# Seven block products for eight in two of the four FFN down units of ten groups

## The reference

```python
def conv_ffn(h, w_up, conv_w, conv_b, w_down, buf):
    z = h @ w_up
    T = z.shape[1]
    zp = jnp.concatenate([buf.astype(z.dtype), z], axis=1)
    zc = conv_b + sum(zp[:, j:j + T] * conv_w[j] for j in range(CONV_W))
    g, a = jnp.split(zc, 2, axis=-1)
    y = (jax.nn.silu(g) * a) @ w_down
    return y, zp[:, -(CONV_W - 1):]
...
    x = x + mix.astype(dt)
    f, new_buf = conv_ffn(rmsnorm(x, norm2), w_up, ffn_conv_w, ffn_conv_b, w_down, conv_buf)
    x = x + f.astype(dt)
```

## Time and profile before

| | |
|---|---|
| median of 3 runs | 2255.8 us (2255.7 to 2257.31) |
| the profiled execution's own time | 2254.32 us |
| its span, first to last instruction | 2252.5 us |
| mean granted TensorE clock | 0.997 |
| TensorE busy in the span | 2227.6 us (99%) |
| matmuls | 18338 |

### The profile page before, as it was taken

The page is one execution under the profiler, slowest core; times in us unless marked ns, Lnnn a source line. Parts: engine busy times, 40 slices in busy tenths (PEclk is TensorE's granted clock), DMA queues, the critical chain, the costliest instruction groups (busy, mean ns, idle before and its releaser), DMA issues.

```text
span 2252.5 us, 44763 instructions
## 1 busy us (share of the span) xinstructions
PE 2227.6 (99%) x18338; PEld 2166.1 (96%) x18338; DVE 876.1 (39%) x1428; ACT 736.5 (33%) x1257; POOL 940.5 (42%) x748
## 2 busy tenths in 40 slices
PE   7999999989999999999999999999999999999999
PEld 7999888988899999999999999999999999999999
DVE  5112457266543532433323333333333333324433
ACT  5222342345443332323323232232322323223321
POOL 5443223332244444444444444444444444444442
PEclk9999999999999999999999999999999999999999
DMA  7532223742133323323233232333323233233323
GB/s 225 124 93 75 60 71 80 134 132 66 55 94 95 96 90 85 89 93 95 93 93 95 84 89 89 93 95 93 95 90 86 87 93 95 93 93 95 92 78 122
DMA packets 325076, 213.61 MB, mean 95 GB/s; under 512 B 12744, under 2 KB 299441, under 8 KB 324081
## 3 DMA queue, kind: packets, MB, share of 16 engines
q1 hardware_dynamic: 322121, 211.27, 33.6%
q10 hardware_dynamic: 2880, 1.26, 0.3%
HBM read 201.37 MB, written 11.49 MB: 94 GB/s over the span
## 4 chain that ended last, share of the span: by engine, by line
PE 92%; issue 3%; POOL 2%; ACT 1%; DVE 1%; DMA 1%; POOLq 0%; SPq 0%; ACTq 0%; DVEq 0%
PE ps L443 56%; PE ps L790 22%; PE ps L691 8%; POOL wlo L1759 1%; PE ps L730 1%; PE ps L750 1%; PE ps L740 1%; DMA xtok<-in_x_prompt 0%; PE ps L560 0%; ACT act_hi L929 0%; PE ps L569 0%; PE ps L568 0%; DMA raw<-in_w_in 0%; PE ps L407 0%; PE ps L858 0%
## 5 line engine op out<-in xcount | busy, mean ns | idle before, releaser
L1759 POOL TENSOR_TENSOR wlo<-raw,whi 128x512 fp32r<-128x512 f32 x696 | 900.4, 1295 | 1252.7 <-ACT whi L898 1252.7
L898 ACT ACTIVATE whi<-raw 128x512 fp32r<-128x512 f32 x712 | 448.0, 631 | 1316.8 <-PE ps L443 854.3
L443 PE MATMUL ps<-h_hi,whi 128*128 128x260 f32 x2816 | 395.7, 283 | 0.0
L443 PE MATMUL ps<-h_lo,whi 128*128 128x260 f32 x2816 | 394.0, 282 | 0.0
L443 PE MATMUL ps<-h_hi,wlo 128*128 128x260 f32 x2816 | 393.2, 282 | 0.0
L443 PEld LDWEIGHTS ps<-h_hi,whi 128*128 128x128 f32 x2816 | 361.1, 188 | 0.4
L443 PEld LDWEIGHTS ps<-h_lo,whi 128*128 128x128 f32 x2816 | 360.9, 188 | 0.0
L443 PEld LDWEIGHTS ps<-h_hi,wlo 128*128 128x128 f32 x2816 | 360.6, 188 | 0.0
L1684 DVE TENSOR_TENSOR xT<-ps,xT 128x520 f32<-128x520 f32 x160 | 111.8, 699 | 287.6 <-PE ps L790 286.4
L1644 DVE TENSOR_TENSOR za<-ps,rs 128x520 f32<-128x520 f32 x44 | 30.8, 700 | 419.4 <-PE ps L443 419.4
L790 PE MATMUL ps<-g_hi,whi 128*128 128x260 f32 x1280 | 181.1, 283 | 0.5 <-DVE xT L1684 0.5
(11 more groups left out here) (327 smaller groups left out, 1973.4 us busy)
## 6 DMA issues: line engine op xcount, KB each, us to landing
raw<-in_w_up SPq DMA_DIRECT2D x88, 1024.0 KB, 5.8
raw<-in_w_down SPq DMA_DIRECT2D x44, 1024.0 KB, 5.0
raw<-in_w_in SPq DMA_DIRECT2D x30, 1024.0 KB, 5.7
raw<-in_w_out SPq DMA_DIRECT2D x64, 256.0 KB, 3.8
x_spill<-xT SPq DMA_DIRECT2D x1, 4160.0 KB, 16.4
xtok<-in_x_prompt SPq DMA_DIRECT2D x4, 1024.0 KB, 8.5
out_y_prompt<-ytok SPq DMA_DIRECT2D x3, 1024.0 KB
xT<-x_spill SPq DMA_DIRECT2D x1, 2860.0 KB, 10.6
```

Of the source, the lines that this page charges most:

```text
L443: mm = nc.tensor.matmul(ps[:, bank + h, 0:NH], w[:, k, c, :], x[:, 4 * c + k, h * NH:(h + 1) * NH], start=(k == 0 and kind == 0 and c == 0 ...
L898: nc.scalar.activation(whi[:, k, :, :], rawq(k, slot), ACT.Copy)\
L1759: nc.gpsimd.tensor_tensor(wlo[:, k, :, :], rawq(k, u), whi[:, k, :, :].bitcast(F32), ALU.subtract).then_inc(w_lo, 1)
```

## The change

In the down units m = 1 and m = 3 of the first ten groups (all but the last) the product of a 512 x 512 weight block with a 512 x 520 activation is seen as a product of 2 x 2 blocks: the 512 channels are split by i, the 512 outputs by r, the tokens in two halves. Instead of eight block products the unit makes seven (`PRODUCTS`, Winograd's form of Strassen's scheme): each is a 256 x 256 weight block, raw or a sum of raw blocks (`WEIGHTS`), times a 256 x 260 activation block, raw or mixed (`mix`). A product is one slot of the ring and 12 matmuls (2 x 2 x 3 kinds) into one of four pairs of PSUM banks A to D. The units m = 0 and m = 2 and all of the last group keep four quarters of 24 matmuls.

- DVE makes three weight sums after the first take of the unit ahead (`weight_sum` 0 to 2), a fourth after the take of the second product, and the low part of product 5 (`weight_low`), which POOL leaves out. It takes the seven products with ten adds (`take_product`); a part that all three later outputs share is gathered in `qacc` over all groups and added once, in the last group's down units.
- DVE also makes the mixed activations (`mix`, `mixed_lo`), ACT their high part (`mixed_hi`).
- In the last loopless part the last group's high and low activations no longer have tiles of their own; they go into slots of `g_hi` and `g_lo` that the last seven-product unit has read (`last_hi`, `last_lo`).
- TensorE's inner loop over down units is written out, and its waits change: `w_hi` and `d_ev` ahead of a product, `w_lo` (for product 5 `w_lo_v`) only ahead of kind 2.

```diff
+PIECES = 7
+SEVEN = (False, True, False, True)
+NS = sum(SEVEN)
+PIECES_OF = [PIECES if x else 4 for x in SEVEN]
+LOWS_OF = [PIECES - 1 if x else 4 for x in SEVEN]
+Q_AT = [sum(PIECES_OF[:m]) for m in range(GC + 1)]
+L_AT = [sum(LOWS_OF[:m]) for m in range(GC + 1)]
+S_AT = [sum(SEVEN[:m]) for m in range(GC + 1)]
...
+    BANK_A, BANK_B, BANK_C, BANK_D = 4, 0, 6, 2
+    PRODUCTS = [(BANK_B, 0), (BANK_D, 5), (BANK_A, 4), (BANK_C, 6), (BANK_B, 2), (BANK_A, 3), (BANK_C, 7)]
+    WEIGHTS = [("a", 0, 0), ("s", 1), ("s", 0), ("s", 2), ("a", 0, 1), ("s", 1), ("a", 1, 1)]
+    SUM_MADE = {1: 2, 2: 2, 3: 3, 5: 4}
+    P_LOW = 5
+    E_SLOT = [0, 5, 4, 6]
...
+        return PRODUCTS[p][0] if SEVEN[m] else (BANK_A, BANK_C)[p % 2]
...
+        def down_unit(m, q0, l0, low0, ev0, read0, read1):
+            for p in range(PIECES_OF[m]):
+                k, bank, last_q = p % 4, down_bank(m, p), last_use(m, p)
+                pe.wait_ge(w_hi, q0 + (Q_AT[m] + p + 1))
+                if last_q is not None:
+                    pe.wait_ge(s("d_ev"), ev0 + (last_q + 1))
+                elif bank == BANK_B:
+                    pe.wait_ge(z_free, read0)
+                elif bank == BANK_D:
+                    pe.wait_ge(z_free, read1)
+                for kind, (w, x) in enumerate(((whi, g_hi), (whi, g_lo), (wlo, g_hi))):
+                    if kind == 2 and SEVEN[m] and p == P_LOW:
+                        pe.wait_ge(s("w_lo_v"), low0 + (S_AT[m] + 1))
+                    elif kind == 2:
+                        pe.wait_ge(w_lo, l0 + (L_AT[m] + (low_index(p) if SEVEN[m] else p) + 1))
+                    for i in range(2):
+                        for j in range(2):
+                            if SEVEN[m]:
+                                mm = nc.tensor.matmul(ps[:, bank + j, 0:NH], w[:, k, 2 * i + j, :],
+                                                      x[:, i, PRODUCTS[p][1], :],
+                                                      start=(kind == 0 and i == 0), stop=(kind == 2 and i == 1))
+                                continue
+                            for h in range(2):
+                                mm = nc.tensor.matmul(ps[:, bank + h, 0:NH], w[:, k, 2 * j + i, :], x[:, i, 2 * j + h, :],
+                                                      start=(kind == 0 and i == 0 and j == 0),
+                                                      stop=(kind == 2 and i == 1 and j == 1))
+                mm.then_inc(w_used, 1)
...
             pe.wait_ge(s("par_ready"), i + 1)
-            pe.wait_ge(s("g_lo"), i * GC)
+            pe.wait_ge(s("g_lo"), i * 6)
             begun(pe)
-            with pe.Fori(0, GC // 2) as mp:
-                for u in range(2):
-                    for _ in down_mm(q0 + mp * 8 + (8 + 4 * u), i * 16 + mp * 8 + (4 * u - 16)):
-                        pass
+            for m in range(GC):
+                down_unit(m, q0 + 8, l0 + 8, i * NS + (GC - NS), i * Q_DOWN + (2 - Q_DOWN), use0 + 3, use0 + 4)
             begun(pe)
             with pe.Fori(1, GC) as jj:
-                up_units(q0 + jj * 8 + 16, use0 + jj * 2, 0)
+                pe.wait_ge(s("d_ev"), i * Q_DOWN)
+                up_units(l0 + jj * 8 + L_DOWN, use0 + jj * 2, 0)
...
+            up_units(l0 + 8 * j, use0, j)
         pe.wait_ge(s("par_ready"), last + 1)
-        pe.wait_ge(s("g_lo"), last * GC)
+        pe.wait_ge(s("g_lo"), last * 6)
         for m in range(GC):
-            for _ in down_mm(q0 + 4 * (U_GRP + m), last * 16 + 4 * m - 16):
-                pass
+            if m == GC - 1:
+                pe.wait_ge(s("t_read"), 2)
+            down_unit(m, q0 + 4 * U_GRP, l0 + 4 * U_GRP, NS * (last - 1) + GC, ev0, use0 + 9, use0 + 10)
             if m == 1:
                 turn_tail()
-        pe.wait_ge(s("g_lo"), NG * GC)
+        pe.wait_ge(s("g_lo"), last * 6 + GC)
+        pe.wait_ge(s("d_ev"), ev0 + Q_DOWN - 1)
         for m in range(GC):
-            for k in down_mm(q0 + 4 * (U_GRP + GC + m), last * 16 + 4 * m, e_hi, e_lo):
+            for k in down_mm(l0 + 4 * U_GRP + L_DOWN + 4 * m, 4 * m):
+                if m == 0 and k == 0:
+                    pe.wait_ge(s("d_ev"), ev0 + Q_DOWN)
                 if 4 * m + k >= 1:
                     turn_y(4 * m + k - 1)
         turn_y(15)
...
+        def seven_hi(q, p, slot, landed, sums_made):
+            if p == 0:
+                act.wait_ge(raw_in[slot], landed)
+            if p in SUM_MADE:
+                act.wait_ge(s("s_made"), sums_made + SUM_MADE[p])
+            act.wait_ge(w_used, q + 1)
+            nc.scalar.activation(ring(whi, p % 4), down_weights(p, slot), ACT.Copy).then_inc(w_hi, 1)
...
+        def take_product(q0, ev0, m, p):
+            dve.wait_ge(w_used, q0 + (Q_AT[m] + p + 5))
+            if SEVEN[m] and p not in (0, 2):
+                dve.wait_ge(s("d_ev"), ev0 + (Q_AT[m] + p))
+            src = pair(down_bank(m, p))
+            acc = qacc[:, 2 * m:2 * m + 2, :]
+            if not SEVEN[m]:
+                x2 = halves(xT[:, 4 * m + p, :])
+                ins = tt(x2, src, x2, add)
+            elif p == 0:
+                tt(acc, src, acc, add)
+                ins = tt(down_tiles(m, 0, 0), src, down_tiles(m, 0, 0), add)
+            elif p == 1:
+                ins = tt(acc, src, acc, add)
+            elif p == 2:
+                tt(down_tiles(m, 0, 1), src, down_tiles(m, 0, 1), add)
+                ins = tt(down_tiles(m, 1, 1), src, down_tiles(m, 1, 1), add)
+            elif p == 3:
+                tt(down_tiles(m, 1, 0), src, down_tiles(m, 1, 0), add)
+                ins = tt(down_tiles(m, 1, 1), src, down_tiles(m, 1, 1), add)
+            else:
+                x2 = down_tiles(m, *((0, 0), (0, 1), (1, 0))[p - 4])
+                ins = tt(x2, src, x2, add)
+            ins.then_inc(s("d_ev"), 1)
+        def weight_sum(made, m, i, landed):
+            if i == 0:
+                dve.wait_ge(raw_in[m % 2], landed)
+            else:
+                dve.wait_ge(s("s_made"), made + (4 * S_AT[m] + i))
+            a11, a12, a21, a22 = (raw_block(m % 2, r, k) for r in range(2) for k in range(2))
+            s1, s2, s3 = (four(sums[:, x, :]) for x in range(3))
+            to, x, y, op = ((s1, a21, a22, add), (s2, s1, a11, sub), (s3, a11, a21, sub), (s2, a12, s2, sub))[i]
+            tt(to, x, y, op).then_inc(s("s_made"), 1)
+        def weight_low(q0, m):
+            dve.wait_ge(w_hi, q0 + (Q_AT[m] + P_LOW + 1))
+            tt(ring(wlo, P_LOW % 4), down_weights(P_LOW, m % 2), ring(whi, P_LOW % 4).bitcast(F32), sub)                .then_inc(s("w_lo_v"), 1)
+        def after_product(q0, ev0, made, raw0, m, p):
+            take_product(q0, ev0, m, p)
+            if SEVEN[m] and p == 1:
+                weight_sum(made, m, 3, None)
+            if SEVEN[m] and p == 2:
+                weight_low(q0, m)
+            if m + 1 < GC and SEVEN[m + 1] and p == PIECES_OF[m] - 4:
+                for i in range(3):
+                    weight_sum(made, m + 1, i, raw0 + 16 * ((m + 1) // 2))
...
+            def mix(i):
+                g0, g1 = gms[i], gms[i + 2]
+                a, b, c, d = (slice(0, NH), slice(NH, N), slice(0, NH), slice(NH, N))
+                then(tt(tmix[:, 0, :], g0[:, b], g0[:, a], sub))
+                then(tt(tmix[:, 1, :], g1[:, d], tmix[:, 0, :], sub))
+                tt(tmix[:, 2, :], g1[:, d], g0[:, b], sub)
+                tt(tmix[:, 3, :], g1[:, c], tmix[:, 1, :], sub).then_inc(s("g_mix"), 1)
+            def mixed_lo(i, before):
+                dve.wait_ge(s("g_hi"), grp * 6 + (0 if before else 4))
+                tt(g_lo[:, i, 4:8, :], tmix[:], g_hi[:, i, 4:8, :].bitcast(F32), sub).then_inc(s("g_lo"), 1)
+            def last_lo(j):
+                dve.wait_ge(s("g_hi"), grp * 6 + (j + 1))
+                tt(e_half(g_lo, j), halves(ems[j][:]), e_half(g_hi, j).bitcast(F32), sub).then_inc(s("g_lo"), 1)
...
+                downs = (with_down and j == 0) or (ends and j == GC - 1)
+                read(n, 0, off, j)
+                read(n, 1, off + 4, j)
+                if downs:
+                    conv(n, 0, j)
+                    for m in range(GC):
+                        for p in range(PIECES_OF[m]):
+                            after_product(qd, ev0, made, raw0, m, p)
+                            if (m, p) == (0, 1):
+                                conv(n, 1, j)
+                            if (m, p) == (0, 2):
+                                gate(n, j)
+                            if ends and m == GC - 1 and p >= 3:
+                                last_lo(p - 3)
+                else:
+                    conv(n, 0, j)
+                    conv(n, 1, j)
+                    gate(n, j)
+                if not ends:
                     lo(n, j)
-                if adds:
-                    for e in range(2, 16):
-                        down(e // 4, e % 4)
-                if not (adds and ends):
-                    lo(n, j)
+                    if j >= 2:
```

(93 more changed lines are left out.)

197 lines of the change are left out of this document (127 added, 70 removed).

## The result

| | before | after |
|---|---|---|
| median of the runs | 2255.75 us (4 runs, 2255.65 to 2257.31) | 2226.85 us (4 runs, 2225.07 to 2229.53) |
| the profiled execution's own time | 2254.32 us | 2225.15 us |
| its span | 2252.5 us | 2223.4 us |
| mean granted TensorE clock | 0.997 | 0.998 |

The ratio is 0.9871, with a 95% interval of 0.9854 to 0.9888: 1.3% faster.

The account below looks back on a forecast made before the run. TensorE, busy 99% of the span, was taken as the bound. From 2254.3 us, - 28.9 - 0.6 + 4.0 + 3.4 gave 2232.2; the median, standing 1.5 us higher, was put at 2234 us, range 2228 to 2245.

Parts of the forecast that it names:

- 240 matmuls less: Twenty seven-product units of 84 matmuls instead of 96, at an unchanged 120.26 ns each: 28.9 us saved.
- the wait at the second-last group's first down unit: TensorE's 0.47 us wait, with restart some 0.6, goes because `e_lo` no longer makes a take late there.
- p6 held up: TensorE waits 0.2 us for banks before the seventh product in each of 20 seven-product units: 4.0 us lost.
- the end wait: Before the last group's down units TensorE waits for four low parts on DVE, slowed by POOL's splits: 3.4 us lost.
- p5's low part is due on DVE at ... 5.73, 0.06 us behind POOL. I take it that it waits: In a seven-product unit, DVE's low part waits for POOL's split, ending at 7.52 us instead of 6.43.
- The first rival: DVE starts product 5's low part before POOL's split, so the units lose nothing: 2230 us, chance 0.22.
- none at all: Sign against the forecast: no TensorE gaps inside the seven-product units, where 0.2 us before the seventh product was expected.
- the pace: New down matmuls assumed to run at the old 120.26 ns each, making a 12-matmul product 1.443 us.
- the rival with a slower pace: Each of 140 products pays a 0.14 us restart, returning 20 us: 2250 us, no change; no gain left had chance 0.06.
- The clock's fall behind the end wait: TensorE drops to half clock after the last group's wait, costing 1.7 us more on any case; chance 3 in 10.
- no cost of the mixes, the sums, the raw slots and the first group's loads: Over a loop pass this added work fits beside TensorE's matmuls and was costed at nothing.
- from 46.18 to 40.8 us: Sign for the forecast: the four down units of a loop pass shorten by this much.

## Why the prediction was wrong in its number

By the terms of the sum, from the profiled executions:

| term | forecast | measured |
|---|---|---|
| 240 matmuls less | -28.9 | -30.5 (10 x 3.05) |
| the wait at the second-last group's first down unit | -0.6 | -0.6 (0.75 us from start to start, less 0.12) |
| p6 held up, 20 units | +4.0 | +0.2 (one gap, at 2135.95, in the last units ahead of the end) |
| the end wait | +3.4 | +3.4 |
| ahead of the FFN, code not touched | 0 | -1.7 (709.77 to 708.10) |
| sum | -22.1 | -29.2 |

The measured terms add up to the difference of the two own times, 2254.32 - 2225.15 = 29.17. The 1.7 us ahead of the FFN are luck and not the change's: the kernel before with its activations moved, whose code ahead of the FFN is the old one, starts the FFN at 708.03 too.

**The step that failed** is "p5's low part is due on DVE at ... 5.73, 0.06 us behind POOL. I take it that it waits". In the loop's 18 units the low part came at 978.34 - 972.61 = 5.73, as forecast to the hundredth, and did not wait (0.68 us): POOL was late, at 5.81 and not 5.67. Its chain starts with p1's take, at 3.18 instead of 3.09. The fourth sum ended at 977.08, and ACT began at 977.20, 0.12 us later, where 0.05 was put; the rest of the way was as put. So two handovers, 0.14 us net, turned the order round, and with it the term: 4.0 us became 0.2.

The 0.2 us are the one unit where the forecast came true: m = 1 of the second-last group, in the loopless part (TensorE starts on p0 at 2127.46):

```profile
2130.54 0.70 DVE L1796 TENSOR_TENSOR qacc<-ps,qacc 128x520 f32<-128x520 f32 x1
2131.87 0.63 ACT L1322 ACTIVATE whi<-sums 128x512 fp32r<-128x512 f32 x1 [2.14 <-DVE sums L1817]
2133.10 1.29 POOL L2044 TENSOR_TENSOR wlo<-raw,whi 128x512 fp32r<-128x512 f32 x1 [2.00 <-ACT whi L1322]
2133.19 1.76 DVE L1822 TENSOR_TENSOR wlo<-sums,whi 128x512 fp32r<-128x512 f32 x1
2136.30 0.71 PE L881 MATMUL ps<-g_hi,whi 128*128 128x260 f32 x4
```

There p1's take comes at 3.08 and POOL at 5.64, the low part at 5.73 waits, and p6 starts at 8.84, 0.23 us late: each within 0.03 us of the forecast (3.09, 5.67, 5.73, 8.87). So the working was right for loopless code and wrong for the loop, which runs the same operations behind the same semaphores. The trace also shows what differs. In the loopless part p1's take and ACT's split of p5 themselves carry the wait that is met last (for TensorE, and for the sum). In the loop a register instruction of the engine's sequencer carries it ahead of them (L1786 for the take, L1321 for the split). The lines below (sequencer, duration in ns as lowest/median/highest, first and last start) have none of these instructions behind the loop:

```profile
L1786 DVEq ALU_OP  x72: 40/40/40, 842.8 to 1954.6; - x72
L1786 DVEq FUSED_REGOPS  x9: 46/46/46, 839.9 to 1925.9; - x9
L1321 ACTq ALU_OP  x126: 35/35/35, 825.6 to 1949.0; - x126
```

The take starts 0.09 us, ACT's split 0.08 us behind the start of such an instruction (975.69 to 975.79 and 977.12 to 977.20). That these are what the forecast lacked fits all 18 units; no run takes them out, so it is read from the traces and not tested by itself.

The first rival, with 0.22, was the case that came in the loop, and "none at all" was named as what would show it. The sum's 20 units also took in the last one, for which the prediction itself has the low part free. What was wrong beside the order was the weight: at a margin of 0.06 us, out of durations known to 0.05, neither order had twice the chance of the other.

**The term that was mis-sized** is the pace, taken over from before. It gave 1.6 us more: 0.1 us a pass comes with the place of `g_hi` (shown), the rest is in the seven-product matmuls. Of the rival with a slower pace (a restart of 0.14 us a product) nothing is seen: a product takes 10.05 / 7 = 1.436 us.

With the order and the pace mended the forecast's own sum gives 2254.3 - 30.5 - 0.6 + 3.4 = 2226.6, and with the 1.7 us that this profile gained by luck ahead of the FFN its own time, 2225. The clock's fall behind the end wait, the rival that was given 3 in 10 at 1.7 us, came in one of the two profiles of the changed kernel, at 2.6.

**What held:** no cost of the mixes, the sums, the raw slots and the first group's loads; the takes beside a split at 0.69 to 0.70 us; the end wait and what it is made of. The rule of the Trainium skill, page "SBUF — State Buffer", section "SBUF: two separate sides", by which the port that DVE and POOL share goes to whichever starts first, for its whole instruction, agrees with both orders: DVE kept it with 0.08 us of lead, POOL with 0.11 (and with 0.09 in the unit at 2127.46). The misreading was who would be first. The line "from 46.18 to 40.8 us" among the signs was a slip: by the forecast's own numbers it is 46.18 - 2.89 + 0.4 = 43.7 (likewise the cover's "40.4 us" is 360 x 0.12026 = 43.3); neither stands in the sum. Measured were 43.12.
